# Mirrored queries in place of a flipped bias, with loads reordered, in a hybrid decoder layer

## The reference

```python
rel = qi[:, None] + BLOCK - kj[None, :]
bias = rel_bias[t5_bucket(rel)]                 # a table of 32 buckets x 8 heads
logits = where((rel >= 0) & (rel < 128), scores + bias, -inf)
m = maximum(max(logits), sink)
p = exp(logits - m); denom = sum(p) + exp(sink - m)
out = (p / denom) @ v
```

## Time and profile before

| | |
|---|---|
| median of three runs | 1971.12 us |
| lowest, highest | 1969.52, 1971.86 us |
| the profiled execution, its own time | 1971.53 us |
| its span in the trace | 1969.7 us |
| mean granted clock of TensorE | 0.989 of full |
| bytes from and to memory in the span | 470 MB read, 27 MB written |

### The profile page before, as it was taken

The page is one execution under the profiler, slowest core; times in us unless marked ns, Lnnn a source line. Parts: engine busy times, 40 slices in busy tenths (PEclk is TensorE's granted clock), DMA queues, the critical chain, the costliest instruction groups (busy, mean ns, idle before and its releaser), DMA issues.

```text
span 1969.7 us, 33296 instructions
## 1 busy us (share of the span) xinstructions
PE 1910.2 (97%) x12224; PEld 1398.8 (71%) x12224; DVE 1303.0 (66%) x3759; ACT 411.8 (21%) x910; POOL 235.6 (12%) x317
## 2 busy tenths in 40 slices
PE   7999999997999999999999999999998999999996
PEld 5677777774999999999999999834333444444442
DVE  2787778774377777775666666645355767777665
ACT  1233332222121122222222222223221100001100
POOL 1212222221010111111111111110100000000000
PEclk8999999998999999999999999999999999999998
DMA  9411100113966778788888989999999999999992
GB/s 311 113 43 43 43 18 35 32 33 144 339 207 228 246 261 269 245 282 278 289 285 283 307 300 304 316 368 381 360 368 382 382 375 356 369 369 367 360 360 72
DMA packets 207682, 498.39 MB, mean 253 GB/s; under 512 B 7716, under 2 KB 14928, under 8 KB 200080
## 3 DMA queue, kind: packets, MB, share of 16 engines
q1 hardware_dynamic: 194016, 449.43, 63.7%
q0 software_dynamic: 11312, 39.85, 8.2%
q10 hardware_dynamic: 2304, 8.39, 1.0%
HBM read 470.24 MB, written 27.41 MB: 253 GB/s over the span
## 4 chain that ended last, share of the span: by engine, by line
issue 40%; PE 29%; DMA 5%; POOL 1%; DVE 1%; POOLq 0%; ACT 0%; DVEq 0%; ACTq 0%
PE ps_unit L1885 29%; DMA out_dram<-y_rows,idx_cur 4%; POOL x_got L1378 1%; DMA x_got<-h_rows,idx_next 0%; PE ps_list L1857 0%; POOL carrier L1374 0%; POOL out_dram L1435 0%; POOLq L1096 0%; POOLq L1290 0%; DVE match L1562 0%; DVE reached L1610 0%; POOL out_dram L1390 0%; POOLq L1426 0%; POOLq L1265 0%; DVE xT L1684 0%
## 5 line engine op out<-in xcount | busy, mean ns | idle before, releaser
L1885 PE MATMUL ps_unit<-xT,w_slot 128*128 128x136 f32 (+6 forms) x3840 | 521.5, 298 | 1.6 <-DVE xT L1684 1.6
L1885 PEld LDWEIGHTS ps_unit<-xT,w_slot 128*128 128x128 f32 x3840 | 516.6, 196 | 2.0 <-issue 2.0
L1915 PE MATMUL ps_unit<-w_slot,xT 128*128 128x512 f32 x704 | 306.7, 594 | 0.0
L1279 DVE STREAM_TRANSPOSE xT<-x_got 32x256 f32<-32x256 f32 x644 | 280.5, 436 | 12.1 <-DMA x_got<-h_rows,idx_next 3.7
L1885 PE MATMUL ps_unit<-act_T,w_slot 128*128 128x136 f32 (+6 forms) x1920 | 261.6, 298 | 0.1
L1885 PEld LDWEIGHTS ps_unit<-act_T,w_slot 128*128 128x128 f32 x1920 | 257.9, 190 | 2.2 <-DVE act_T L1659 1.5
L1915 PEld LDWEIGHTS ps_unit<-w_slot,xT 128*128 128x128 f32 x704 | 132.8, 190 | 163.0 <-issue 163.0
L1675 DVE STREAM_TRANSPOSE y_rows<-yT 32x256 f32<-32x256 f32 x372 | 162.1, 436 | 55.0 <-ACT yT L1481 50.1
L928 PE MATMUL ps_c<-hT,w_in_sb 128*128 128x128 f32 x1536 | 182.1, 279 | 4.3 <-DMA w_in_sb<-in_w_in_dram 4.3
L928 PEld LDWEIGHTS ps_c<-hT,w_in_sb 128*128 128x128 f32 x1536 | 177.3, 194 | 9.6 <-DMA w_in_sb<-in_w_in_dram 5.2
L1374 POOL TENSOR_TENSOR carrier<-carrier 128x1 f32<-128x1 f32 x64 | 14.5, 227 | 1319.1 <-issue 610.8
(11 more groups left out here) (294 smaller groups left out, 1790.5 us busy)
## 6 DMA issues: line engine op xcount, KB each, us to landing
w_slot<-in_w_dram SPq DMA_DIRECT2D x192, 2048.0 KB, 12.1
b_row<-in_b_dram SPq DMA_DIRECT2D x11, 1024.0 KB, 12.9
w_in_sb<-in_w_in_dram SPq DMA_DIRECT2D x6, 1024.0 KB, 12.0
b_row<-in_b_dram SPq DMA_DIRECT2D x11, 512.0 KB, 15.1
x_in<-in_x_dram SPq DMA_DIRECT2D x8, 512.0 KB, 3.5
x_res<-in_x_dram SPq DMA_DIRECT2D x8, 512.0 KB, 4.7
out_dram<-x ACTq DMA_DIRECT2D x8, 512.0 KB, 5.1
h_rows<-h ACTq DMA_DIRECT2D x8, 512.0 KB, 3.1
```

What stands on the lines that cost most here:

```text
L1279: last = nc.vector.transpose(out[c * Q:(c + 1) * Q, :, tokens], rows.rearrange("p (k c j) -> p k c j", c=P // Q, j=Q)[:, :, c, :])
L1885: last = pe.matmul(ps_unit[p % RING][:, u, 0:n], w, moving[:, k, 0:n], start=(k == 0), stop=(k == KD - 1))
L1915: last = pe.matmul(ps_hid[c], xT[:, k, 0:P], w_slot[:, c, k, :], start=(k == 0), stop=(k == KD - 1))
```

## The change

Queries of a block are processed in reverse order of partitions: ACT writes `qT` with its columns mirrored, so scores, probabilities and the bias have their rows in the order in which the slanted load brings it. DVE writes `attnT` and `attn_ss` mirrored back. The flip on PE, the flipped identity in the constants and DVE's two copies are gone; the constants for the bias are loaded for 32 partitions only, and the mask in `keys_in` is made from a count along the columns plus the partition's number. The slanted load is now two, one for each half of the keys, straight into `bias_all` and `bias_prev`, in pieces of 128 values. ACT issues them, after its square of q and k, and also the eleven vector loads (`rows`, ahead of its first square) and the store of the table. SP issues three of the convolution's loads right behind the q/k/v part and its bias, and the other three after x's second rows. `add_bias` of block 0 on DVE and the start of POOL's blocks wait for the two slanted loads; PE waits for the two halves of `w_out` at separate places.

```diff
-C_FLIP = C_MASK + REL_W
-C_W = C_FLIP + P
+C_W = C_MASK + REL_W

...
-    c[:, C_FLIP:C_FLIP + P] = np.eye(P)[::-1]

...
         attn_sq = qk_sq[:, 0:AW].rearrange("p (c q) -> p c q", c=CC)
-        rel_const = x1[:, 0:2 * REL_W + P]
+        rel_const = x1[0:NBUCKET, 0:2 * REL_W]
         vector_rows = h2[0:42, 0:P]
...
-        out_w_loaded = sem("out_w_loaded")
+        conv_out_w_loaded = sem("conv_out_w_loaded")
+        attn_out_w_loaded = sem("attn_out_w_loaded")

...
-        bias_turned = sem("bias_turned")
-        bias_flipped = sem("bias_flipped")

...
         early = [
-            (rel_const, const[:, C_HOT:C_W]),
+            (cst[:], const[:, 0:C_HOT]),
             (rel_bias_sb[:], rel_bias),
+            (rel_const, const[0:NBUCKET, C_HOT:C_W]),
             (sink_row[:], sinks[0].partition_broadcast(P)),
-            (cst[:], const[:, 0:C_HOT]),
+        ]
+        rows = [
             (vector_rows[0:8, :], norm_mix.rearrange("o (k p) -> (o k) p", p=P)),
...
         ]
-        all_early, all_late = 16 * len(early), 16 * len(late)
+        all_early, all_late = 16 * (len(early) + len(rows)), 16 * len(late)
...
+
+            def load_conv_w(pair):
+
+                for j in range(3):
+                    part = slice(j * CW + 2 * pair * P, j * CW + 2 * (pair + 1) * P)
+                    sp.dma_start(w_in_sb[:, :, part], w_rows[:, :, part]).then_inc(conv_w_loaded[pair], 16)
+
             for i in range(2):
                 part = slice(i * KD // 2, (i + 1) * KD // 2)
                 sp.dma_start(w_in_sb[:, part, QKV0:IN_W], w_rows[:, part, QKV0:IN_W]).then_inc(qkv_w_loaded[i], 16)
             sp.dma_start(b_qkv_row[:], b_in[0, QKV0:IN_W].partition_broadcast(P)).then_inc(qkv_b_loaded, 16)
+            load_conv_w(0)
             wait(sp, x_normed, 0)
             sp.dma_start(x_in[:], x_rows[P:2 * P, :]).then_inc(x_loaded.sem, 16)
-            sp.wait_ge(rel_made, 1)
-            sp.dma_start(rel_rows, rel_row).then_inc(rel_stored, 16)
-
-            def load_conv_w(pair):
-
-                for j in range(3):
-                    part = slice(j * CW + 2 * pair * P, j * CW + 2 * (pair + 1) * P)
-                    sp.dma_start(w_in_sb[:, :, part], w_rows[:, :, part]).then_inc(conv_w_loaded[pair], 16)
-
-            sp.wait_ge(rel_stored, 16)
-            slanted = bass.AP(tensor=rel_rows.tensor, offset=0, ap=[[1, P], [REL_W, NH], [1, 2 * P]])
-            sp.dma_start(probs[:], slanted).then_inc(bias_loaded, 16)
-            for pair in range(CC // 2):
-                load_conv_w(pair)
-            sp.dma_start(w_out_sb[:, 0:CC, :], w_out[0, 0:CW, :].rearrange("(k p) n -> p k n", p=P)).then_inc(out_w_loaded, 16)
+            load_conv_w(1)
+            sp.dma_start(w_out_sb[:, 0:CC, :], w_out[0, 0:CW, :].rearrange("(k p) n -> p k n", p=P)).then_inc(conv_out_w_loaded, 16)
             for i in range(2):
                 first = CW + i * AW // 2
                 sp.dma_start(w_out_sb[i * HD:(i + 1) * HD, CC:, :],
-                             w_out[0, first:first + AW // 2, :].rearrange("(h d) n -> d h n", d=HD)).then_inc(out_w_loaded, 16)
+                             w_out[0, first:first + AW // 2, :].rearrange("(h d) n -> d h n", d=HD)).then_inc(attn_out_w_loaded, 16)
             for dst, src in late:
...
             pool.wait_ge(early_loaded, all_early)
-            pool.wait_ge(bias_flipped, 2)
+            pool.wait_ge(bias_loaded, 32)
             def add_taps_pool(t, c):
...
 
+            for dst, src in rows:
+                act.dma_start(dst, src).then_inc(early_loaded, 16)
             square_x(0)
             norm_x(0)
+            act.wait_ge(rel_made, 1)
+            act.dma_start(rel_rows, rel_row).then_inc(rel_stored, 16)
             act.wait_ge(vectors_ready, 1)
             nc.scalar.activation(q_scale_col[:], q_norm_col, ACT.Copy, scale=HD ** -0.5).then_inc(scale_made, 1)
             square_qk(0)
+            act.wait_ge(rel_stored, 16)
+            act.wait_ge(cleared, 6)
+            for dst, first in ((bias_all[:, :, P:2 * P], P), (bias_prev[:], 0)):
+                slanted = bass.AP(tensor=rel_rows.tensor, offset=first, ap=[[1, P], [REL_W, NH], [1, P]])
+                act.dma_start(dst, slanted).then_inc(bias_loaded, 16)
             act.wait_ge(scale_made, 1)
-            act.wait_ge(cleared, 6)
             def one_block(t, more):
...
                                      ACT.Copy, scale=k_norm_col)
-                nc.scalar.activation(qT[:].rearrange("p h q -> p (h q)"), ps_s[:, 0:512],
+                nc.scalar.activation(qT[:, :, ::-1], ps_s[:, 0:512].rearrange("p (h q) -> p h q", h=NH // 2),
                                      ACT.Copy, scale=q_scale_col[:]).then_inc(qT_ready.sem, 1)
...
             norm_qk(0)
-            dve.wait_ge(bias_turned, 1)
-            nc.vector.tensor_copy(bias_prev[:], ps_heads[:, :, 0:P]).then_inc(bias_flipped, 1)
-            nc.vector.tensor_copy(bias_all[:, :, P:2 * P], ps_heads[:, :, P:2 * P]).then_inc(bias_flipped, 1)
-            dve.wait_ge(bias_flipped, 2)
             nc.vector.tensor_copy(tri_b[:], cst[:, C_TRI:C_TRI + P])
-            nc.vector.tensor_tensor(keys_in[:, 1, :], cst[:, C_TRI:C_TRI + P], ident, ALU.add).then_inc(keys_made, 1)
+            nc.vector.tensor_scalar(keys_in[:, 1, :], cst[:, C_IOTA:C_IOTA + P], cst[:, C_PART:C_PART + 1], P - 0.5,
+                                    ALU.add, ALU.is_lt).then_inc(keys_made, 1)
             dve.wait_ge(keys_made, 1)
...
                 wait(dve, scored[0], t)
-                if not first:
+                if first:
+                    dve.wait_ge(bias_loaded, 32)
+                else:
                     dve.wait_ge(bias_switched, 1)
...
                 wait(dve, av_done, t)
-                nc.vector.tensor_tensor(attnT[:].rearrange("p (a b) q -> p a b q", b=2),
+                nc.vector.tensor_tensor(attnT[:].rearrange("p (a b) q -> p a b q", b=2)[:, :, :, ::-1],
                                         ps_c[:, 0, :].rearrange("p (a b q) -> p a b q", b=2, q=P),
                                         attn_g_col.rearrange("p (b a) -> p a b", a=2).unsqueeze(3).broadcast_to([P, 2, 2, P]),
                                         ALU.mult).then_inc(attnT_ready.sem, 1)
                 wait(dve, attn_squared, t)
-                nc.vector.tensor_reduce(attn_ss[:], attn_sq.rearrange("p c q -> p q c"), AX_X,
+                nc.vector.tensor_reduce(attn_ss[:, ::-1], attn_sq.rearrange("p c q -> p q c"), AX_X,
                                         ALU.add).then_inc(attn_joined.sem, 1)
...
             project_kv(0)
-            pe.wait_ge(bias_loaded, 16)
             pe.wait_ge(vectors_ready, 1)
-            for i in range(4):
-                last = pe.matmul(ps_s[:, i * 512:(i + 1) * 512], rel_const[:, 2 * REL_W:], probs[:, 2 * i:2 * i + 2, :].rearrange(
-                    "p h k -> p (h k)"), start=True, stop=True)
-            last.then_inc(bias_turned, 1)
             project_conv(0, 0, (0, 1))
             def one_block(t, more):
 
                 project_conv(t, 0, (2,))
                 project_conv(t, 1, (0,))
                 wait(pe, qk_normed, t)
-                pe.wait_ge(bias_flipped, 2)
                 for i in range(NH // 2):
...
                 wait(pe, biased[1], t)
-                pe.wait_ge(out_w_loaded, 48)
+                pe.wait_ge(conv_out_w_loaded, 16)
                 mix_conv((0, 1))
...
                 wait(pe, attnT_ready, t)
+                pe.wait_ge(attn_out_w_loaded, 32)
                 for n in range(2):
```

## The result

The change does not gain 11 us; it loses a little. The changed kernel's median is 1975.53 us (22 runs, 1967.85 to 1989.11, a spread that run 14 comes back to) against 1970.92 for the kernel before (22 runs on the same chip): a ratio of 1.0029 [1.0017, 1.0041], 4.6 us slower. The profiled execution took 1983.12 us, with a span of 1981.3 against 1969.7. The head of its page: PE's busy time is 2 us less than before, and the span 11.6 us more.

What follows compares the result with a forecast made beforehand. The start was taken as bound by when SP issues loads, the later blocks by PE. The terms summed to -11.05 us, the rest 0: 1960.5 from the profiled 1971.53, 1960.1 for the median; range 1957.3 to 1966.0.

Steps and rivals of the forecast that it cites:

- Part 4: Block 0's new wait for the slanted bias loads: landing at 38.4, first bias add from 49.45 to 38.4, -11.05 us.
- rival C: Slower than before: slanted 512-byte pieces alternate with SP's 4 KB ones, bias lands at 56, +7 us, 1978; 4%.
- Part 1: At the start, eleven small loads move from SP's queue to ACT's: q starts at 11.4 instead of 13.25, -1.85 us.
- Part 2: The q, k and v matmuls: clock holds, end at 21.8 (24.7 if it falls), instead of 26.59.
- Part 3: First convolution weights issued earlier land at 23.9 instead of 34.36; flip (3.60 us) goes; scores ready at 38.0.
- Part 5: Later loads: second convolution weights just in time, 0 to 1 us risk; x_res covered; splitting w_out's wait gives 0.
- Part 6: Mirrored writes of qT and attnT in eight blocks: 0 us, covered by PE even at twice the time.
- The sum: All parts over the whole run: -11.05 us and the rest 0, giving 1960.1.

Runs made afterwards that it cites:

- run 14: The changed kernel itself, measured once more with no edit: 1971.08 us, ratio 1.0008 to the kernel before.
- run 13: The changed kernel with four small dummy matmuls added on PE at the start, same code as run 9, measured again: 1962.06 us, ratio 0.9951 to the kernel before.
- run 9: The changed kernel with four small dummy matmuls added on PE at the start: 1960.59 us, ratio 0.9946 to the kernel before.
- run 4: The changed kernel with SP, not ACT, issuing both slanted loads, ahead of the second convolution weights: 1964.62 us, ratio 0.9969 to the kernel before.
- run 5: Run 4 with four small dummy matmuls added on PE at the start: 1960.65 us, ratio 0.9943 to the kernel before.
- run 7: Run 4 with PE waiting for all of w_out ahead of the first mixing matmul: 1969.84 us, ratio 0.9997 to the kernel before.
- run 11: Run 4 with two small dummy matmuls added on PE at the start: 1964.08 us, ratio 0.9959 to the kernel before.
- run 1: The changed kernel with SP holding w_out back until both slanted loads have landed: 1964.6 us, ratio 0.9968 to the kernel before.
- run 16: Run 13's code with ACT issuing the slanted loads later, after qk_rstd, and w_out loaded in four column quarters: 1964.61 us, ratio 0.9959 to the kernel before.
- run 8: The kernel before with only the first three convolution loads issued earlier, ahead of x's second rows: 1975.27 us, ratio 1.0027 to the kernel before.

## Why the prediction was wrong

**The failed step is Part 4, the price of a slanted piece.** I took 78 to 109 ns for each of 128, "if each takes turns with a 1 KB piece of SP's", and a landing at 38.4. Beside 1 KB pieces the price is about right for the second load (74 and 84 ns measured; landings of 39.4 to 40.5 when ACT issues by 25, or w_out is held back). But the changed kernel's second load met w_out's 4 KB rows, at 306 ns a piece: the landing was 57.4. This is rival C, whose sum (56, 1978) came out nearly, and which I gave 4%. I dismissed it because "1 KB pieces are what SP holds at that time". Three things were overlooked. SP issues the second weights and w_out in one stretch, with w_out in the queue at 27.12, before ACT's loads; and those go one after the other in ACT's queue, so that the second only begins about when the first has landed, 10 us later, when w_in's pieces run out. And C's price of 157 ns for a 4 KB row came from 416 GB/s, where attention's half moves at about 205, slanted load or not (208 in the kernel before's row above), so that a row of it takes 16 x 4096 / 205 = 320 ns. C's cost was right in sum by luck: only half of the pieces paid, each about 1.4 times what C took for it. The first load of the pair fits no price: it takes 9.0 to 11.8 us in nine profiles, where 64 pieces at 78 ns and the fixed 2 us would be 7; what the rest is stays open.

**Part 1** gave q at 11.4; it was 14.18. The vectors, on ACT's queue beside SP's weights, land at 10.09 where they landed by 8.69 (the row below is from the kernel before), and the table load of 1.28 us stands behind ACT's eleven issues, so the square starts at 5.72, where 5.4 was my upper bound.

```profile
8.69 0.17 DVE L745 COPY sink_slots<-sink_row 128x8 f32<-128x8 f32 x1 [2.85 <-DMA h<-in_k_norm_dram]
```

**Part 2** took the clock as held. It was 0.50 at 12 to 14 in the changed kernel's profile, and held in run 13's; k and v end at 26.15 and 23.6. That end decides when ACT issues, and so between the kinds of runs; the clock and the start of q both go into it (in run 9's late profile the clock was 1.00 at 12 to 14 and fell only then). In the runs without a profile that is inferred from their times and clocks.

**Part 3** nearly held: the weights come without a wait at 25.98, and L929 takes 7.31 (7.5). Where PE does wait for them they land at 25.1 (run 4) and 26.6 (run 13), 1.2 and 2.7 us later than the 23.9 of the forecast. The scores were ready to be added at about 38.4 (38.0): DVE's wait begins then. From Parts 1 to 3 alone the gain would have been 11 us, and runs 4 and 5 show it, 11.6 and 10.4 at the mixer's end. **Part 5** said that the split of w_out's wait gives 0; it saves 5.2 us as soon as the rest is early (run 7). **Part 6** held: qT takes 680 ns in the median as before, attnT 677 against 681, and the block is 52.78 us long from scores to scores. The 54.48 us that I took for a block was not one: in the kernel before, too, the scores at 102.72 are followed by those at 155.51, 52.79 later. Mirrored writes cost nothing.

```profile
155.51 2.00 PE L1009 MATMUL ps_s<-kT,qT 64*128 64x256 f32 x16
```

**The sum** also left out the experts. They lose 2.4 to 2.9 us in any version with the shorter PE program (rows of 571 us above, runs 4, 5 and 11), which no row of before could tell. And waiting costs more than the wait: after 18 us at rest PE's clock is 0.50, and the 48 matmuls that took 5.62 us take 8.04. Of run 4's 11.6 us, 6 reach the run (5.0 in the profile); 2.9 are the gap and 3.0 the group behind it at the lower clock. Another 2.3 are lost before the second list, 1.7 of them in a group of 18.81 us (17.13 before), with the clock at 0.52 from 480 to 483; some 1.5 are won back later, unexplained.

## What to carry over

Before you move a load to a second queue, list what the first queue will hold all the time until the load lands, by **length of piece**, and price each piece of yours at the time of one of theirs. Short strided pieces belong ahead of long rows, in the same line (run 4), or the long rows are held back or cut (runs 1 and 16). Then look at what decides the order, and whether it hangs on a race of a microsecond or two: one profile of a kernel whose runs spread tells of one of them. And look whether the long rows are slow in themselves: the price of your piece goes with it.

## What was not expected of the hardware

- Two queues share the DMA engines by pieces: a 512-byte piece costs about 30 ns alone, 74 to 84 beside 1 KB pieces, 277 to 306 beside the 4 KB rows of w_out, most of them of its slow half (next point).
- The half of w_out that is loaded in two parts of 64 partitions each is slow even with no slanted load about. Two stretches in which it is the one large load, of run 1 and of run 13 (last number: GB/s), against 350 to 400 for the loads into 128 partitions:

```profile
50.00:55.00 5.00, 3.08 (x20) 2.13 (x19) 3.96 (x8) 0.95 (x3) 4.92 (x7) 1.00 1.04 209
```
```profile
50.00:55.00 5.00, 3.09 (x26) 2.79 (x25) 3.24 (x9) 1.65 (x5) 4.84 (x8) 1.00 1.06 196
```

- PE waits 2.4 to 2.9 us between two groups of matmuls in the second expert, depending on a few instructions more or less 500 us earlier.
- SP is held for 10.5 to 12.6 us by issuing three loads of 1 MB behind 3 MB that are still under way (run 8, run 13), so that a short store behind them is that late (run 8).
